# A decoder step on one Trainium2 core: the order of TensorE's work inside each attention step

## The chip, the cores and the metric

The program runs on one core of a Trainium2 chip. The metric is device time in microseconds (us), as the median of several executions. Three executions of the kernel before took 2781.90, 2783.97 and 2784.48 us, so the median is 2783.97 us.

TensorE appears as two rows in the profile: PE is the matrix product that streams through the array, PEld is the load of the stationary operand ahead of it. DVE is VectorE, ACT is ScalarE, POOL is GpSimd, SP issues transfers.

## The reference, cut to what matters

Two layers are computed for a prompt of 1024 tokens and for 8 short sample sequences of 8 tokens. The change touches only the attention of the second layer. In it, each of 16 heads of the prompt computes

```
s = q @ k.T * Dh**-0.5 - slope * distance        # causal, three dilation patterns
p = exp(s - max(s));  den = sum(p)
o = (p @ v) / den
```

and each sample sequence does the same for 8 new queries against a cache of 2048 keys and values, of which the kernel reads ten tiles of 128 positions each (`cache_k`, `cache_v`). The three patterns are folded into one additive bias (log of how often a key is counted), so one softmax per head is enough.

## The kernel before, in words

**Steps.** The 16 heads are taken as 8 pairs, and each pair's 1024 queries in 8 blocks of 128. That makes 64 prompt steps, numbered n = 0 to 63, with qb = n mod 8 the query block. Step n handles (qb + 1) * 128 key columns for both heads, so steps grow from qb = 0 to qb = 7. Two more steps (64, 65) finish the pipeline, and five steps (-5 to -1) run ahead of it. The first four of them are slipped between the matrix products of the q/k/v projection (line 483).

**The pipeline of the prompt.** In step n TensorE computes the scores of block n (`scores`, line 2419, 64 rows of the array for each head). VectorE adds the bias and takes the maximum (line 2679). ScalarE takes the exponential (`probs`, line 2585, once for each head, e = 0 and 1). In step n+1 TensorE turns the probabilities (transposes, line 2459, in units of up to four 128x128 blocks), and VectorE copies each turned unit out of PSUM (line 2638, `att_pt`). In step n+2 TensorE multiplies them with the values (`pv`, lines 2501 and 2505, the array split into two halves of 64 columns), ScalarE copies a row of reciprocal sums (line 2607), and VectorE writes the result (line 2710, `att_out`). `pv(n-2)`, called in step n, waits for two things of VectorE's step n-1: for the last turned unit of block n-2 (`t_out`), and for `att_out` of block n-3, which is the last instruction that VectorE has in step n-1 (`a_ox`).

**The samples.** One sample sequence is spread over eight steps, s = 0 to 7, and s = (qb + 5) mod 8 until the last pair, where s = 6 and 7 move to steps 58 and 60. Its key tiles are turned (line 2444) in two units each. `K_AT` says at which unit each s begins. ScalarE copies every unit out (line 2561, `smp_kt`, room for two tiles). A turned tile is multiplied with the queries (`tile_scores`, line 2472, the array split into four parts of 32 columns), at the places that `SCORED` names by (s, f). In s = 7 the ten value tiles are used (`sample_pv`, line 2526, also split in four), at the places of `WEIGHED`.

**Order.** Nothing is scheduled by a planner: every engine runs the list that is written out. A step has four phases, f = 1 to 4, and the units of a step (`turns`) are dealt out two to a phase. TensorE's list in a phase is: `scores` (f = 1 only), the phase's transposes, `pv` (f = 1 only), `tile_scores`, `sample_pv`.

**Banks.** A turned unit needs one PSUM bank, and the unit is not started before the copy of the unit that had the bank last. Two banks are always there. Two more are the second halves of the scores' banks: `rest` (line 2311) allows them in steps with qb under 4 in every phase, and in the others from phase 3, after VectorE has read the scores. The scores of the next step in turn wait for the copies out of those two banks before they write their second half.

**Memory.** Key and value tiles come by DMA into ten or twelve buffers. A buffer is loaded again when its key tile has been turned or its value tile has been used.

Of the kernel before, what the change touches and what calls it, by code (L numbers as in the profile page):

```python
# [25 lines left out]
QT = SEQ // P  # L26
# [106 lines left out]
def build(nc, a):  # L133
# [2114 lines left out]
    NSLOT = HP * QT  # L2248
# [10 lines left out]
    def sample_slot(n):  # L2259
        b, s = divmod(n + LEAD, 8)  # L2260
        if n >= min(LAST_S.values()) or b >= DB or slot_of(b, s) != n:
            b, s = DB - 1, next((s for s, x in LAST_S.items() if x == n), None)
        return (b, s) if s is not None else (None, None)

    K_AT = (0, 4, 8, 11, 14, 17, 20, 20, 20)
    SCORED = {(0, 2): (0,), (0, 3): (1,), (1, 2): (2,), (1, 3): (3,), (2, 2): (4,), (3, 1): (5,), (3, 3): (6,), (4, 2): (7,),
              (5, 1): (8,), (5, 3): (9,)}
    WEIGHED = {(7, 1): range(1, 5), (7, 2): range(5, 8), (7, 4): (8, 9, 10, 0)}

    def turns(n):  # L2270

# [18 lines left out]
    def by_act(unit):  # L2290

        return unit[0] not in ("p", "s") or unit[0] == "s" and unit[2] == 1

    def phase(n, f):

        nt = len(turns(n))
        return range(2 * f - 2, min(2 * f, nt) if f < 4 else nt)
# [10 lines left out]
    for n in SLOTS:  # L2308
        for f in range(1, 5):
            for i in phase(n, f):  # L2310
                rest = () if n < 0 else (2,) if n >= NSLOT else (2, 3) if n % QT < 4 or f >= 3 else ()
                x = min((0, 1) + rest, key=lambda b: last_use[b])
                last_use[x] = len(TB_)
                TC_.append(TB_.count(x) + 1)
                TB_.append(x)
# [85 lines left out]
    def att_pe(pe):  # L2401
# [129 lines left out]
        def step(n, f):  # L2531
            b, s = sample_slot(n)
            if 0 <= n < NSLOT and f == 1:
                scores(n)
            for i in phase(n, f):
                turn(n, i)
            if 2 <= n and f == 1:
                pv(n - 2)
            for t in SCORED.get((s, f), ()):
                tile_scores(b, t)  # L2540
            sample_pv(b, WEIGHED.get((s, f), ()))

        return step

# [35 lines left out]
    def s9_act(act):  # L2580
        def probs(n, e):
            W = (n % QT + 1) * P
            k = 2 * (n % 4) + e
            act.wait_ge(a_red, 2 * n + e + 1)
            act.activation(SX[n % 2][:, e, 0:W], SX[n % 2][:, e, 0:W], ACT.Exp, bias=NBM[:, k:k + 1], scale=-1.0,
                           accum_out=DEN[:, k:k + 1]).then_inc(a_p, 1)

        for n in SLOTS[N_RUN + LEAD:]:
            b, s = sample_slot(n)
            mine = [i for i, u in enumerate(turns(n)) if by_act(u)]  # L2590
            for i in mine[0:2]:
                take_act(act, n, i)
            if 0 <= n < NSLOT:
                probs(n, 0)
            for i in mine[2:3]:
                take_act(act, n, i)
            if 0 <= n < NSLOT:
                probs(n, 1)
            for i in mine[3:]:
                take_act(act, n, i)  # L2600
            if n == NSLOT + 1:
                act.wait_ge(a_red, 2 * NSLOT)
                for k in range(3):
                    out1_hi(act, k)
            if 2 <= n:
                act.wait_ge(a_o, n - 1)
                act.activation(RS[:, n % 2, :], PS[:, 6, P:2 * P], ACT.Copy).then_inc(a_rc, 1)
            if s == 5:
                act.wait_ge(b_mn, b + 1)
                act.activation(SS[:, :], SS[:, :], ACT.Exp, bias=NMN[:, 0:1], scale=-1.0,  # L2610
                               accum_out=DNS[:, 0:1]).then_inc(b_p, 1)
            if n == slot_of(DB - 1, 7) + 2:
                act.wait_ge(b_oc, DB)
                for e in range(2):
                    act.activation(ODUP[:, :, e, :], OALL[:, :].rearrange("p (b d) -> p b d", b=DB),
                                   ACT.Copy).then_inc(b_du, 1)
            if n == NSLOT - 5:
                split_hi(act, B_OUT1)

    def s9_dve(dve):  # L2620
# [28 lines left out]
        def piece(b, i):  # L2649
            c, w = (0, 2 * P) if i < 5 else (2 * P, DS)  # L2650
            k = 0 if i == 5 else i
            dve.wait_ge(b_sc, 5 * b + k + 1)
            dve.tensor_tensor_reduce(SS[:, i * 256:i * 256 + w], PS[:, 7, c:c + w], BSS[:, i * 256:i * 256 + w],
                                     -(DH ** -0.5), 3.0e38, ALU.add, ALU.min, NM6[:, i:i + 1]).then_inc(b_red, 1)
# [10 lines left out]
        for n in SLOTS:  # L2665
            b, s = sample_slot(n)
            units = turns(n)
# [19 lines left out]
            if n == slot_of(DB - 1, 7) + 1:  # L2687
                weigh(DB - 1)
            for f in range(1, 5):
                for i in range(2 * f - 2, min(2 * f, len(units)) if f < 4 else len(units)):  # L2690
                    if units[i][0] == "qk" or not by_act(units[i]):
                        take(n, i)
                for t in SCORED.get((s, f), ()):
                    if t % 2:
                        piece(b, t // 2)
                    if t == 1:
                        piece(b, 5)
            if s == 5:
                dve.wait_ge(b_red, 6 * b + 6)
                dve.tensor_reduce(NMN[:, :], NM6[:, :], AX.X, ALU.min).then_inc(b_mn, 1)  # L2700
# [285 lines left out]
```

## Time and profile before

| | us |
|---|---|
| median of three executions | 2783.97 |
| profiled execution, its own time | 2784.42 |
| span of the profile | 2782.6 |
| attention, first `scores` to the last product of `pv` | 1504.2 to 1929.1 |

The profiled execution took 1.8 us more than its span; it is 0.45 us above the median. The whole program keeps TensorE busy for 98% of the span. The attention is 425 us of it, of which the first pair of heads takes 55.6 us, the next six together 320.5 us, and the last pair with the two closing steps 48.8 us. Times in the trace are microseconds from the start of the span. An entry such as [0.17 <-issue] behind a row is idle time of that engine right before it, with what ended it; "issue" means that nothing the profile shows was waited for.

### The profile page before, as it was taken

The page shows a single profiled execution, that of the slowest core. Times are in us where ns is not written, and L with a number is a line of the kernel's source. Part 1 is how long each engine was busy: PE and PEld are TensorE (multiplying, and loading weights), DVE is VectorE, ACT ScalarE, POOL GpSimd, SP SyncE. Part 2 cuts the span into 40 slices and gives each one's busy share as a digit, 9 for nine tenths or more (in the row PEclk, how much of TensorE's full clock was granted, in tenths as well). Part 3 has the DMA queues.
Part 4 walks back from the last instruction along what each step waited for, and adds up shares of the span by engine and source line. Part 5 has one row for each costly group of instructions (what it writes and reads, how often), then busy time and mean ns, then how long its engine had stood idle before and what let it go on. Part 6 is the DMA issues. An engine that isn't in the chain of part 4 may idle for free.

```text
span 2782.6 us, 54662 instructions
## 1 busy us (share of the span) xinstructions
PE 2739.0 (98%) x23577; PEld 2618.6 (94%) x23577; DVE 1737.1 (62%) x2858; ACT 946.1 (34%) x1690; POOL 118.5 (4%) x220
## 2 busy tenths in 40 slices
PE   7999999999999999999999999999999999999998
PEld 7999999999999999999997777777999999999998
DVE  5754536877777776755512566556377767776676
ACT  5543513322222222422223555555232222222222
POOL 1010000000000000000011111110000000000000
PEclk9999999999999999999999999999999999999999
DMA  5120220111111111232356776873101111111112
GB/s 200 37 80 18 67 92 30 32 60 47 47 46 46 46 46 47 85 112 85 95 176 212 237 258 220 266 253 129 61 16 46 46 46 47 46 47 46 53 55 80
DMA packets 126381, 254.53 MB, mean 91 GB/s; under 512 B 7617, under 2 KB 88725, under 8 KB 125632
## 3 DMA queue, kind: packets, MB, share of 16 engines
q1 hardware_dynamic: 112944, 189.26, 21.0%
q0 software_dynamic: 11888, 57.25, 5.9%
q8 instruction: 189, 3.10, 0.5%
q10 hardware_dynamic: 1312, 4.52, 0.5%
q14 instruction: 48, 0.39, 0.0%
HBM read 222.98 MB, written 28.02 MB: 90 GB/s over the span
## 4 chain that ended last, share of the span: by engine, by line
PE 92%; DVE 4%; ACT 2%; DMA 1%; issue 1%; POOL 0%; ACTq 0%; POOLq 0%; DVEq 0%
PE psum L1574 30%; PE psum L1629 17%; PE psum L483 14%; PE psum L224 11%; PE psum L1549 3%; PE psum L2444 3%; PE psum L2501 2%; PE psum L2419 2%; PE psum L2459 2%; PE psum L2472 1%; PE psum L2526 1%; DMA x_natural<-in_x_prompt 1%; DMA cache_tile<-in_cache_k 1%; PE psum L592 1%; PE psum L2448 1%
## 5 line engine op out<-in xcount | busy, mean ns | idle before, releaser
L1810 DVE TENSOR_TENSOR x_res<-x_res,psum 128x544 f32<-128x544 f32 x352 | 250.5, 719 | 155.5 <-PE psum L1629 155.5
L483 PE MATMUL psum<-w_hi,h_hi 128*128 128x256 f32 (+1 forms) x1152 | 327.2, 284 | 1.0 <-ACT qkv_tok L2074 1.0
L483 PE MATMUL psum<-w_hi,h_lo 128*128 128x256 f32 (+1 forms) x1152 | 323.6, 281 | 0.0
L483 PE MATMUL psum<-w_lo,h_hi 128*128 128x256 f32 (+1 forms) x1152 | 323.0, 280 | 0.0
L1629 PE MATMUL psum<-ffn_hi,ffn_unit_hi 128*128 128x272 f32 x1408 | 292.6, 289 | 1.8 <-DVE x_res L1810 1.5
L1629 PE MATMUL psum<-ffn_lo,ffn_unit_hi 128*128 128x272 f32 x1408 | 291.5, 288 | 0.0
L1629 PE MATMUL psum<-ffn_hi,ffn_unit_lo 128*128 128x272 f32 x1408 | 290.7, 288 | 0.0
L1574 PE MATMUL psum<-h_hi,ffn_unit_lo 128*128 128x272 f32 x1280 | 265.2, 288 | 0.0
L1574 PE MATMUL psum<-h_lo,ffn_unit_hi 128*128 128x272 f32 x1280 | 264.8, 288 | 0.0
L1574 PE MATMUL psum<-h_hi,ffn_unit_hi 128*128 128x272 f32 x1280 | 264.5, 288 | 0.0
L1629 PEld LDWEIGHTS psum<-ffn_hi,ffn_unit_hi 128*128 128x128 f32 x1408 | 220.7, 188 | 3.2 <-DVE x_res L1810 3.2
L1629 PEld LDWEIGHTS psum<-ffn_lo,ffn_unit_hi 128*128 128x128 f32 x1408 | 220.8, 188 | 0.0
L1629 PEld LDWEIGHTS psum<-ffn_hi,ffn_unit_lo 128*128 128x128 f32 x1408 | 220.7, 188 | 0.0
L483 PEld LDWEIGHTS psum<-w_hi,h_hi 128*128 128x128 f32 (+1 forms) x1152 | 215.1, 187 | 4.6 <-issue 2.2
L483 PEld LDWEIGHTS psum<-w_lo,h_hi 128*128 128x128 f32 (+1 forms) x1152 | 215.2, 187 | 0.0
L483 PEld LDWEIGHTS psum<-w_hi,h_lo 128*128 128x128 f32 (+1 forms) x1152 | 215.0, 187 | 0.0
L1574 PEld LDWEIGHTS psum<-h_hi,ffn_unit_hi 128*128 128x128 f32 x1280 | 201.0, 188 | 0.0
L1574 PEld LDWEIGHTS psum<-h_hi,ffn_unit_lo 128*128 128x128 f32 x1280 | 200.7, 188 | 0.0
L1574 PEld LDWEIGHTS psum<-h_lo,ffn_unit_hi 128*128 128x128 f32 x1280 | 200.6, 189 | 0.0
L1574 PE MATMUL psum<-ffn_t_hi,ffn_unit_lo 128*128 128x272 f32 x960 | 198.6, 288 | 0.0
L1574 PE MATMUL psum<-ffn_t_hi,ffn_unit_hi 128*128 128x272 f32 x960 | 198.6, 288 | 0.0
L1574 PE MATMUL psum<-ffn_t_lo,ffn_unit_hi 128*128 128x272 f32 x960 | 198.5, 288 | 0.0
(385 smaller groups left out, 5307.1 us busy)
## 6 DMA issues: line engine op xcount, KB each, us to landing
cache_tile<-in_cache_k SPq DMA_DIRECT2D x64, 512.0 KB, 8.5
cache_tile<-in_cache_v SPq DMA_DIRECT2D x64, 512.0 KB, 11.9
w_raw<-in_w_ffn_gate SPq DMA_DIRECT2D x22, 1024.0 KB, 5.1
w_raw<-in_w_ffn_up SPq DMA_DIRECT2D x22, 1024.0 KB, 5.1
w_raw<-in_w_ffn_down SPq DMA_DIRECT2D x22, 1024.0 KB, 4.9
w_raw<-in_w_in_att SPq DMA_DIRECT2D x12, 1024.0 KB, 7.1
w_raw<-in_w_in_rec SPq DMA_DIRECT2D x10, 1024.0 KB, 5.0
park_x<-x_res POOLq DMA_DIRECT2D x2, 4368.0 KB, 13.3
```

The source lines that it names most:

```text
L224: mm = pe.matmul(PS[:, bank + c, 0:n], st[slot][:, wc:wc + P], mv[:, k, c * CW:c * CW + n], start=(i < NCH), stop=(i >= 3 * NCH * nk - NCH))
L483: mm = pe.matmul(PS[0:n, bank, 0:BW], st[:, k, w:w + n], mv[slot][:, k * BW:(k + 1) * BW], start=(k == 0 and x == 0) if used is None else ...
L592: pe.matmul(PS[:, bank, 0:n], wt[:, j, :], XC[j % 2][:, c * CW:c * CW + n], start=True, stop=True).then_inc(g_in, 1)
L1549: mm = pe.matmul(PS[:, 2 * s + c, 0:CC], st[slot][:, k * BW + f * P:k * BW + (f + 1) * P], mv[:, k, t * TH + c * CC:t * TH + (c + 1) * CC] ...
L1574: mm = pe.matmul(PS[:, 2 * s + c, 0:CC], st[i % NU][:, k * P:(k + 1) * P], mv[:, k0 + k, t * TH + c * CC:t * TH + (c + 1) * CC], start=(fr ...
L1629: mm = pe.matmul(PS[:, 2 * s + c, 0:CC], st[(w0 + m // 2) % NU][:, x:x + P], mv[:, f, t * TH + c * CC:t * TH + (c + 1) * CC], start=(n < 2 ...
L1810: dve.tensor_tensor(x, x, pset(dset(g, i)), ALU.add).then_inc(s_res, 1)
L2419: mm = pe.matmul(PS[:, 2 * e + c // 512, 0:min(512, W - c)], q[p % 2][e * DH:(e + 1) * DH, qb * P:(qb + 1) * P], k[p % 2][e * DH:(e + 1) * ...
L2444: mm = pe.transpose(to[:, h * P:(h + 1) * P], TILE[BUF[j]][:, hp * P:(hp + 1) * P], ident[:, :])
L2448: mm = pe.transpose(to[:, t * P:(t + 1) * P], (QN, KN)[c // 2][:, 4 * (c % 2) + t, :], ident[:, :])
L2459: mm = pe.transpose(to[:, (k - c) * P:(k - c + 1) * P], SX[x % 2][:, e, y * P:(y + 1) * P], ident[:, :])
L2501: pe.matmul(PS[e * DH:(e + 1) * DH, 6, 0:P], VN[p % 2][:, x, e * DH:(e + 1) * DH], PT[:, m % 2, e * (qb + 1) + x, :], start=(x == 0), stop ...
```

## The change

In every phase TensorE now does the column-split products first (`pv`, `tile_scores`, `sample_pv`) and the transposes last. Every tile is scored in phase 1 of the step after the one that turned it, two tiles at a time. All the key units are turned in s = 0 to 4, four a step. Value tiles are used in two groups instead of three. The two further banks are allowed from phase 2. ScalarE takes the exponential of head 0 before its first two copies (it was after them), and VectorE does the maxima of the sample scores before its copies of turned units.

```diff
-    K_AT = (0, 4, 8, 11, 14, 17, 20, 20, 20)
-    SCORED = {(0, 2): (0,), (0, 3): (1,), (1, 2): (2,), (1, 3): (3,), (2, 2): (4,), (3, 1): (5,), (3, 3): (6,), (4, 2): (7,),
-              (5, 1): (8,), (5, 3): (9,)}
-    WEIGHED = {(7, 1): range(1, 5), (7, 2): range(5, 8), (7, 4): (8, 9, 10, 0)}
+    K_AT = (0, 4, 8, 12, 16, 20, 20, 20, 20)
+    SCORED = {(1, 1): (0, 1), (2, 1): (2, 3), (3, 1): (4, 5), (4, 1): (6, 7), (5, 1): (8, 9)}
+    WEIGHED = {(7, 1): range(1, 6), (7, 3): (6, 7, 8, 9, 10, 0)}
...
-                rest = () if n < 0 else (2,) if n >= NSLOT else (2, 3) if n % QT < 4 or f >= 3 else ()
+                rest = () if n < 0 else (2,) if n >= NSLOT else (2, 3) if n % QT < 4 or f >= 2 else ()
...
                 scores(n)
-            for i in phase(n, f):
-                turn(n, i)
             if 2 <= n and f == 1:
                 pv(n - 2)
             for t in SCORED.get((s, f), ()):
                 tile_scores(b, t)
             sample_pv(b, WEIGHED.get((s, f), ()))
+            for i in phase(n, f):
+                turn(n, i)
...
+            if 0 <= n < NSLOT:
+                probs(n, 0)
             for i in mine[0:2]:
                 take_act(act, n, i)
             if 0 <= n < NSLOT:
-                probs(n, 0)
-            for i in mine[2:3]:
-                take_act(act, n, i)
-            if 0 <= n < NSLOT:
                 probs(n, 1)
-            for i in mine[3:]:
+            for i in mine[2:]:
                 take_act(act, n, i)
...
-                for i in range(2 * f - 2, min(2 * f, len(units)) if f < 4 else len(units)):
-                    if units[i][0] == "qk" or not by_act(units[i]):
-                        take(n, i)
                 for t in SCORED.get((s, f), ()):
                     if t % 2:
                         piece(b, t // 2)
                     if t == 1:
                         piece(b, 5)
+                for i in range(2 * f - 2, min(2 * f, len(units)) if f < 4 else len(units)):
+                    if units[i][0] == "qk" or not by_act(units[i]):
+                        take(n, i)
```

TensorE, kernel before, step 15 (qb = 7) behind its scores, and the scores of step 16. `cache_tile` rows are key tiles being turned, `att_scores` rows are probabilities being turned, `att_pt` and `att_diag` are `pv`, `smp_kt` is `tile_scores`:

```order
L2444 MATMUL psum<-ident,cache_tile_191 128x128 x8
L2501 MATMUL psum<-att_pt,att_v_218 64x128 x12
L2505 MATMUL psum<-att_diag,ones 64x128 x2
L2444 MATMUL psum<-ident,cache_tile_182 128x128 x4
L2459 MATMUL psum<-ident,att_scores_207 128x128 x4
L2472 MATMUL psum<-smp_kt,smp_q_blocks 32x128 x8
L2459 MATMUL psum<-ident,att_scores_207 128x128 x10
L2419 MATMUL psum<-att_k_hi_203,att_q_hi_199 128x128 x2
L2419 MATMUL psum<-att_k_lo_205,att_q_hi_199 128x128 x2
L2419 MATMUL psum<-att_k_hi_203,att_q_lo_201 128x128 x2
```

TensorE, changed kernel, the same step, then the scores and the `pv` of step 16 (line numbers are one lower):

```order
L2500 MATMUL psum<-att_pt,att_v_218 64x128 x12
L2504 MATMUL psum<-att_diag,ones 64x128 x2
L2471 MATMUL psum<-smp_kt,smp_q_blocks 32x128 x16
L2443 MATMUL psum<-ident,cache_tile_191 128x128 x8
L2443 MATMUL psum<-ident,cache_tile_183 128x128 x8
L2458 MATMUL psum<-ident,att_scores_207 128x128 x14
L2418 MATMUL psum<-att_k_hi_203,att_q_hi_199 128x128 x2
L2418 MATMUL psum<-att_k_lo_205,att_q_hi_199 128x128 x2
L2418 MATMUL psum<-att_k_hi_203,att_q_lo_201 128x128 x2
L2500 MATMUL psum<-att_pt,att_v_218 64x128 x14
L2504 MATMUL psum<-att_diag,ones 64x128 x2
```

The eight transposes that stood between `scores` and `pv` are gone from there, the two kinds of transposes are one row of 30, and one more key unit and one more tile product are in the step.

ScalarE, kernel before, step 15: copies of turned key units (`smp_kt`), the exponentials of both heads, and the row of reciprocal sums:

```order
L2561 ACTIVATE smp_kt<-psum 128x512 x2
L2585 ACTIVATE att_scores_208,att_den<-att_scores_208,att_max 128x1024
L2561 ACTIVATE smp_kt<-psum 128x512
L2585 ACTIVATE att_scores_208,att_den<-att_scores_208,att_max 128x1024
L2607 ACTIVATE att_rden_rows<-psum 128x128
```

ScalarE, changed kernel, the same step:

```order
L2584 ACTIVATE att_scores_208,att_den<-att_scores_208,att_max 128x1024
L2560 ACTIVATE smp_kt<-psum 128x512 x2
L2584 ACTIVATE att_scores_208,att_den<-att_scores_208,att_max 128x1024
L2560 ACTIVATE smp_kt<-psum 128x512 x2
L2604 ACTIVATE att_rden_rows<-psum 128x128
```

The first exponential now stands ahead of all copies; the second still stands between the copies of the second and the third key unit, and one copy has been added behind it.

## Rows read from the trace of the kernel before

**Rows 1.** The page: busy us of the engines, share of the span, instructions.

```profile
PE 2739.0 (98%) x23577; PEld 2618.6 (94%) x23577; DVE 1737.1 (62%) x2858; ACT 946.1 (34%) x1690; POOL 118.5 (4%) x220
```

**Rows 2.** Stretches of attention: length, busy times, granted clock, DMA share, GB/s.

```profile
1504.20:1559.80 55.60, 50.50 (x613) 37.98 (x609) 28.60 (x83) 29.95 (x67) 10.02 (x19) 0.94 0.93 302
1559.80:1880.30 320.50, 318.36 (x4149) 245.56 (x4148) 192.85 (x547) 171.37 (x402) 53.58 (x100) 1.00 0.73 245
1880.30:1929.10 48.80, 45.05 (x557) 35.02 (x556) 36.01 (x90) 25.47 (x57) 6.05 (x10) 1.00 0.46 158
```

**Rows 3.** Waits in the attention, 1504 to 1929: us in total, times, longest.

```profile
PEld psum L2444 <- issue: 17.6, 64, 2.9
...
PEld psum L2501 <- issue: 11.0, 62, 0.6
...
PEld psum L2472 <- ACT smp_kt L2561: 5.6, 16, 1.8
```

**Rows 4.** Timeline of PEld, one step with qb = 7: start, length, operation, count.

```profile
1711.73 0.19 PEld L2419 LDWEIGHTS psum<-att_k_hi,att_q_hi 64*128 64x128 f32 x2 [0.20 <-issue]
...
1713.32 0.86 PEld L2444 LDWEIGHTS psum<-ident,cache_tile 128*128 128x128 f32 x8 [0.36 <-issue]
1714.34 1.29 PEld L2501 LDWEIGHTS psum<-att_pt,att_v 128*64 128x64 f32 x24 [0.17 <-issue]
...
1717.04 0.38 PEld L2472 LDWEIGHTS psum<-smp_kt,smp_q_blocks 128*32 128x32 f32 x16 [0.17 <-issue]
1717.62 1.07 PEld L2459 LDWEIGHTS psum<-ident,att_scores 128*128 128x128 f32 x10 [0.20 <-issue]
1718.86 0.19 PEld L2419 LDWEIGHTS psum<-att_k_hi,att_q_hi 64*128 64x128 f32 x2 [0.17 <-issue]
...
1719.34 0.86 PEld L2444 LDWEIGHTS psum<-ident,cache_tile 128*128 128x128 f32 x8
```

**Rows 5.** Timeline of ACT in the same step.

```profile
1714.01 1.09 ACT L2561 ACTIVATE smp_kt<-psum 128x512 f32<-128x512 f32 x2 [2.27 <-PE psum L2444]
1714.99 1.15 ACT L2585 ACTIVATE att_scores<-att_scores,att_max 128x1024 f32<-128x1024 f32 x1
...
1717.21 1.14 ACT L2585 ACTIVATE att_scores<-att_scores,att_max 128x1024 f32<-128x1024 f32 x1
...
1718.34 0.26 ACT L2607 ACTIVATE att_rden_rows<-psum 128x128 f32<-128x128 f32 x1
```

**Rows 6.** Timeline of DVE at the end of the same step.

```profile
1718.31 1.62 DVE L2638 COPY att_pt<-psum 128x512 f32<-128x512 f32 x3
1719.85 0.28 DVE L2710 TENSOR_TENSOR att_out<-psum,att_rden_rows 128x128 f32<-128x128 f32 x1
```

**Rows 7.** Groups on ACT, 1504 to 1929: exponentials of two widths.

```profile
L2585 ACT ACTIVATE att_scores<-att_scores,att_max 128x1024 f32<-128x1024 f32 x16 | 18.3, 1145 | 0.0
...
L2585 ACT ACTIVATE att_scores<-att_scores,att_max 128x768 f32<-128x768 f32 x16 | 14.9, 931 | 6.3 <-DVE att_max L2679 6.3
```

**Rows 8.** Timeline of DVE, end of step 56 and start of step 57.

```profile
1885.39 1.89 DVE L2638 COPY att_pt<-psum 128x512 f32<-128x512 f32 x3 [3.34 <-PE psum L2459]
...
1888.20 0.28 DVE L2710 TENSOR_TENSOR att_out<-psum,att_rden_rows 128x128 f32<-128x128 f32 x1
```

**Rows 9.** Timeline of PEld, end of step 56 and start of step 57.

```profile
1884.64 1.34 PEld L2459 LDWEIGHTS psum<-ident,att_scores 128*128 128x128 f32 x12
...
1887.31 0.19 PEld L2419 LDWEIGHTS psum<-att_k_hi,att_q_hi 64*128 64x128 f32 x2 [0.17 <-issue]
...
1887.86 0.20 PEld L2459 LDWEIGHTS psum<-ident,att_scores 128*128 128x128 f32 x2
1888.60 0.99 PEld L2501 LDWEIGHTS psum<-att_pt,att_v 128*64 128x64 f32 x18 [0.54 <-DVE att_pt L2638]
```

**Rows 10.** Timeline of PEld, steps 2 and 3.

```profile
1517.02 0.20 PEld L2505 LDWEIGHTS psum<-att_diag,ones 128*64 128x64 f32 x4 [0.77 <-POOL att_diag L2765]
...
1526.54 0.50 PEld L2444 LDWEIGHTS psum<-ident,cache_tile 128*128 128x128 f32 x3 [2.88 <-issue]
```

## The prediction

> **What bounds the kernel now.** The page comes first: TensorE is busy for 98% of the span, the others for 62% or less [rows 1], so time moves only where TensorE's own list gets shorter or where it waits. The second view cuts the attention into stretches. The six middle pairs of heads take 320.5 us with TensorE busy for 318.4 and the granted clock at 1.00; VectorE works 60% and ScalarE 53% of it [rows 2]. The third view is the waits: there is hardly one on another engine. What idles is the weight load with the releaser "issue", 11.0 us in 62 places before `pv` alone [rows 3]. The timeline of one step shows where: between two transposes of a row there is no gap, but wherever the array's split changes (64-row scores, full transposes, 64-column `pv`, 32-column tile products) there is one of 0.17 to 0.20 us [rows 4]. So the attention is bound by TensorE's instructions plus the changes of split, and the change is about the latter. The Trainium skill says in "TensorEngine Tiling (Array Packing)", Key Properties, that changing the tiling mode, not just the tile, drains TensorE; the trace agrees with its 0.17 us.
>
> **What it saves.** I counted the changes of split in both orders of TensorE, from the first score product to the last product of `pv`: 374 before, 243 after, about 49 and 31 per pair. By their kinds (0.17 where a transpose or `pv` ends, 0.20 where a tile product or the scores end, [rows 4]) the 131 that go are worth 23.3 us. In the steps ahead of step 0 seven more go, 1.3 us. Sum -24.6. The step from scores to `pv` is new in 62 places. The trace has only the step from scores to transposes, whose load idles 0.36 us at the widest block, most of that behind the product that is still streaming [rows 4]. I price it like the one it replaces; at no cost the sum would be 12 lower, at twice 0.20 it would be 12 higher.
>
> A tile product now comes a step after its transposes, so it no longer waits for ScalarE's copy: 5.6 us in 16 waits, of which 16 x 0.17 is drain that stays counted above, -2.9 [rows 3], and I estimate -1.4 for the like in the lead steps. The number of products, transposes, copies and exponentials is unchanged, and so are the bytes moved.
>
> **What it adds: waits.** The handovers first. A transpose takes 0.107 us (8 in 1.02 less the 0.17 of drain), a unit of four 0.43 [rows 4]. Its copy starts 0.69 us after the unit does, on ScalarE (1713.32 to 1714.01) as on VectorE (1717.62 to 1718.31). ScalarE copies a unit every 0.49 and the last is done after 0.60; its exponential with its reading takes 1.13 for 1024 columns [rows 5] and 0.11 less for every 128 fewer [rows 7]. VectorE copies one every 0.60, half a unit in 0.34, and `att_out` takes 0.28 [rows 6, 8]. From the end of `att_out` to the waiting `pv` it is 0.12 [rows 8, 9].
>
> *Seventh unit.* With four banks the seventh transposed unit needs the bank of the third key unit. Take 0 as the start of the first key unit. ScalarE copies two, from 0.69 to 1.67, then runs its second exponential to 2.80, and only then copies the third, done at 3.40. TensorE, with no other work between, is there at 6 x 0.43 = 2.58: 0.82 us of wait at qb = 7, 0.71 at qb = 6, 0.60 at qb = 5. The eighth unit (qb = 7) waits for the fourth copy, 3.89, another 0.06. Before, a tile product and the pair of transposes ahead of `pv` lay between and there was no such wait.
>
> *pv at qb = 0.* The eighth unit (two blocks) ends at 4.10, the drain 0.17 and the narrow scores 0.48 [rows 4] bring TensorE to `pv` at 4.75. VectorE copies the seventh from 4.09 and the eighth from 4.69, and `att_out` ends at 5.31, with 0.12 of handover: 0.68 of wait. Before, eight transposes (1.02 us) stood ahead of `pv` and covered it. Queued behind the waiting `pv` is all the rest of the step.
>
> *pv at qb = 1.* In the step before, all four units are probabilities and all go to VectorE. From their start it needs 0.69 + 4 x 0.60 + 0.06 for the least of the sample scores + 0.28 + 0.12 = 3.55. TensorE needs 16 x 0.107 + 0.17 + 0.55 (the scores of 256 columns, [rows 9]) = 2.43: 1.12 of wait. Step 57 of the kernel before shows this very wait: it has no key units ahead of `pv`, only two transposes, and `pv` stood 0.54 us for VectorE [rows 9].
>
> *The rest, by the same working.* At qb = 1 the two query units hold their banks until ScalarE and then VectorE have read them, 0.59; `pv` at qb = 2 then waits 0.75 for VectorE's long list of that step; at qb = 4 the second half of the scores and `pv` wait 0.32 together, at qb = 5 0.05. Per pair: 0.82 + 0.06 + 0.71 + 0.60 + 0.68 + 1.12 + 0.59 + 0.75 + 0.32 + 0.05 = 5.7 us, against about 18 x 0.175 = 3.1 us that the same pair saves in drains. Six full pairs give 34.2, the first pair from its step 4 on 2.6, the last in its first two steps 1.8: +38.6. In the closing steps, without key units, waits like these are there already (3.75 of the 48.8 us are not busy, [rows 2]); I leave them even.
>
> **Start and transfers.** In step 2 `pv` waits for POOL [rows 10], whose list is held by the last stores of the projection. That moment doesn't move, so what TensorE saves between the projection and it is lost, and slightly more work stands behind it: +3. The next wait, 2.88 us at step 3 [rows 10], is for the first key tile of the second sample. Its buffer is freed by the first value tile, and now about 1.6 us more work lies between the two: -2. The same spacing, 7.8 us in place of 6.2, holds for every later sample, so SP's loads, with the DMA engines 73% busy [rows 2], are not later than now.
>
> **Sum.** -24.6 - 4.3 - 2 + 38.6 + 3 = +10.7 on the profiled execution's own 2784.42, so 2795, 11 above the median of 2783.97. VectorE then works no more than before and still has slack on average; what costs is the order.
>
> **Rivals.**
> *Drains only.* If copies and waits stay hidden, the kernel gains 24.6 + 4.3 + 2 less 3 and comes to 2757. The drains [rows 4] and the 98% [rows 1] speak for it. Against it stands step 57 [rows 9], and the handovers above are read from rows and leave the copies no room. The Trainium skill ("TensorEngine Tiling (Array Packing)") stands on both sides: its rule on mode switches makes every removed switch a gain and would lead here, while its section PSUM Bottleneck says that tiling speeds up TensorE but not the emptying of PSUM. Chance 0.10; together with halfway cases in which under 60% of the waits appear (38.6 x 0.6 = 23.2, so 2780 or less: under 2778.4), faster has 0.16.
> *A draw.* With 60 to 85% of the waits (a copy that starts earlier than the step I read, or waits that overlap: one wait moves VectorE's start of the next step and softens the next) the sum is -5 to +5: 2779 to 2789. Chance 0.19.
> *The clock falls.* In the first stretch, with its long waits, the granted clock is 0.94 against 1.00 later [rows 2]. If the new idle time, 5.7 us of waits in 55, did the same everywhere, 6% of the 320 us would add 19: 2814. Against it: the last stretch has 3.75 us not busy in 48.8 and its clock is 1.00. Chance 0.04.
> *The new split costs double.* Scores to `pv` at 0.40 in place of 0.20: 2807. Nothing in the rows says so; 0.06.
> The forecast case itself (2789 to 2802) has 0.55.
>
> **How the numbers follow.** A measurement of this kernel tells about 0.2%, 5.6 us, from no change. Faster by more than that takes the first rival with its halfway cases, 0.16; within it the draw, 0.19; slower the forecast and the last two, 0.65. The range of 8 in 10 runs from 2777 to 2807: it leaves out most of the faster cases and the clock. The likeliest case's own range is 2789 to 2802.
>
> **What would show it.** In the changed profile: weight loads of `pv` with a releaser on VectorE (`att_out` or `att_pt`), worst at qb = 1 with about 1.1 us, then qb = 2 and 0; probability transposes at qb = 5 to 7 that wait for ScalarE's `smp_kt` by 0.6 to 0.8; "issue" gaps fewer by a third; no wait of tile products; six middle pairs of 56 us each instead of 53.4; the granted clock 1.00 in them. Middle pairs under 53 us would refute the handovers; pairs at 50 would mean the drains are all there is.

## The result and the profile after

The changed kernel takes 2806.48 us (median of 6 runs, 2802.86 to 2807.82), the kernel before 2784.52 (6 runs beside it, 2781.90 to 2787.15). The ratio is 1.0077 with a 95% interval of 1.0068 to 1.0087: 22 us slower. The forecast was 2795.0 in a range of 2777 to 2807, so direction and cause were foreseen, and the loss was put at half its size.

The profiled execution took 2806.05 us, its span 2804.2. The page answers to [rows 1]: the share of TensorE fell from 98% to 97%, with the same number of instructions.

```profile
PE 2730.4 (97%) x23577; PEld 2621.8 (93%) x23577; DVE 1739.2 (62%) x2858; ACT 947.4 (34%) x1690; POOL 118.8 (4%) x220
```

The stretches of the changed kernel, with the columns of [rows 2]: the first pair of heads, the six middle pairs, the fourth pair alone, and the last pair with the closing steps. They are cut at the first score product of a step.

```profile
1502.12:1557.15 55.03, 47.93 (x608) 37.55 (x607) 28.65 (x82) 30.19 (x68) 9.24 (x17) 0.97 0.92 298
1557.15:1899.53 342.38, 312.94 (x4148) 248.14 (x4148) 194.61 (x547) 171.88 (x402) 53.73 (x100) 1.00 0.68 228
1672.42:1728.55 56.13, 51.90 (x692) 41.27 (x691) 32.45 (x92) 28.62 (x67) 9.24 (x17) 1.00 0.70 235
1899.53:1949.91 50.38, 43.70 (x545) 33.74 (x544) 36.04 (x89) 24.25 (x54) 6.07 (x10) 1.00 0.44 153
```

The fourth pair of the kernel before:

```profile
1665.86:1718.86 53.00, 52.94 (x692) 40.92 (x692) 32.14 (x92) 28.56 (x67) 9.22 (x17) 1.00 0.74 250
```

The whole loss lies in the middle pairs: 342.4 against 320.5 us, +21.9, where TensorE has 29 us without a product in place of 2. I call the fourth pair regular, because nothing but the written order delays it: 56.13 against 53.00, +3.1. Six times that is 18.8. The other 3.1 are stops that come only in some pairs (below), net of those that the kernel before had. The granted clock is 1.00 in all middle pairs, as before.

The waits in the attention, as in [rows 3] (total us, times, longest):

```profile
PEld psum L2500 <- DVE att_pt L2635: 25.4, 26, 1.8
...
PEld psum L2458 <- issue: 18.7, 35, 0.9
...
PEld psum L2500 <- issue: 9.0, 26, 1.3
PEld psum L2443 <- issue: 8.0, 29, 2.1
```

Key transposes had 17.6 us of gaps in 64 places [rows 3] and now have 8.0 in 29: most of that is drains that went. New at this size is the first row, `pv` waiting for VectorE. In the kernel before it is 2.3 us in three places, all in the last pair and the closing steps:

```profile
PEld psum L2501 <- DVE att_pt L2638: 2.3, 3, 1.4
```

The wait of tile products for ScalarE, 5.6 us [rows 3], has no row any more. Over all lines the "issue" gaps went from 326 to 245, but their sum from 71.7 to 75.4 us, since some of them are waits for a bank and not drains.

Which waits these are shows in the weight loads of TensorE in the fourth pair. First the steps with qb = 7 and 0, to be held against [rows 4]:

```profile
1719.80 0.19 PEld L2418 LDWEIGHTS psum<-att_k_hi,att_q_hi 64*128 64x128 f32 x2 [0.17 <-issue]
...
1720.65 0.19 PEld L2418 LDWEIGHTS psum<-att_k_hi,att_q_hi 64*128 64x128 f32 x2 [0.33 <-DVE att_pt L2635]
...
1721.54 1.29 PEld L2500 LDWEIGHTS psum<-att_pt,att_v 128*64 128x64 f32 x24 [0.36 <-issue]
...
1724.23 1.73 PEld L2443 LDWEIGHTS psum<-ident,cache_tile 128*128 128x128 f32 x16 [0.20 <-issue]
1725.93 0.90 PEld L2458 LDWEIGHTS psum<-ident,att_scores 128*128 128x128 f32 x8
1727.70 0.69 PEld L2458 LDWEIGHTS psum<-ident,att_scores 128*128 128x128 f32 x6 [0.86 <-issue]
1728.55 0.19 PEld L2418 LDWEIGHTS psum<-att_k_hi,att_q_hi 64*128 64x128 f32 x2 [0.17 <-issue]
...
1729.73 0.34 PEld L2500 LDWEIGHTS psum<-att_pt,att_v 128*64 128x64 f32 x6 [0.77 <-DVE att_pt L2635]
```

Six units of transposes run without a gap, then the seventh stands for 0.86 us, and in the next step `pv` stands for 0.77. The new step from scores to `pv` idles 0.36, exactly what scores to transposes idled [rows 4]. ScalarE in the same step, against [rows 5]:

```profile
1722.92 1.15 ACT L2584 ACTIVATE att_scores<-att_scores,att_max 128x1024 f32<-128x1024 f32 x1 [3.13 <-DVE att_max L2676]
...
1724.93 1.09 ACT L2560 ACTIVATE smp_kt<-psum 128x512 f32<-128x512 f32 x2 [0.76 <-PE psum L2443]
1725.90 1.15 ACT L2584 ACTIVATE att_scores<-att_scores,att_max 128x1024 f32<-128x1024 f32 x1
...
1727.03 1.08 ACT L2560 ACTIVATE smp_kt<-psum 128x512 f32<-128x512 f32 x2
```

The third key unit is copied from 1727.03 on, behind the second exponential, and the seventh transposed unit begins at 1727.70, 3.47 us after the first; the working gave 3.40. Then `pv` at qb = 1 and 2 of the same pair, the two worst places:

```profile
1680.09 1.76 PEld L2500 LDWEIGHTS psum<-att_pt,att_v 128*64 128x64 f32 x32 [1.25 <-DVE att_pt L2635]
...
1686.67 0.23 PEld L2500 LDWEIGHTS psum<-att_pt,att_v 128*64 128x64 f32 x4 [0.92 <-DVE att_pt L2635]
```

What was not foreseen shows in step 13. TensorE is in the second half of its scores, between products that wait for nothing:

```profile
1590.24 0.19 PEld L2418 LDWEIGHTS psum<-att_k_hi,att_q_hi 64*128 64x128 f32 x2 [0.32 <-ACT smp_kt L2560]
1592.75 0.19 PEld L2418 LDWEIGHTS psum<-att_k_lo,att_q_hi 64*128 64x128 f32 x2 [2.32 <-issue]
```

Packets of the queues between 1586 and 1592 us (packets, MB, share of the 16 DMA engines):

```profile
q1 hardware_dynamic: 482, 1.43, 100.9%
q8 instruction: 1, 0.02, 1.4%
```

The DMA engines are full with cache tiles, and one packet of the instruction queue lies among them. It starts at 1590.0 and takes 1.4 us: it is under way when the stop begins (1590.4) and over 1.3 us before TensorE goes on. At step 37 TensorE stops for 1.28 us between its scores and `pv`, the DMA engines are full there too (103.2% for q1 between 1755 and 1762), and TensorE goes on 1.7 us after the end of such a packet. That alone proves little: the six middle pairs have 34 such packets, one in about 10 us, and 17 of them lie among full DMA engines, but only these two stand beside a stop of over a microsecond. One that starts at 1707.1, in the regular fourth pair, stops nothing. The kernel before has 34 too, 16 of them among full DMA engines, and no stop of that length. Step 3 is another matter: its 2.08 us are a wait for a key tile, for the product's row there names the DMA transfer of `cache_tile` as its releaser.

The Trainium skill ("Runtime: NRT & Kernel Launch", the note on `TENSOR_LOAD` in The ~15µs preamble/postamble breakdown) says that instructions are fetched on their own, without an instruction for it. The trace agrees in that only the packet shows.

### The profile page after: what moved, and what is told of

Same layout as the page of the kernel before. It is cut to its first block, busy times and chain, and to the rows that moved or that the text cites. A ratio compares the mean times of both kernels' runs of the same rounds, so it can differ in the third digit from the quotient of the medians.

```text
span 2804.2 us, 54662 instructions
## 1 busy us (share of the span) xinstructions
PE 2730.4 (97%) x23577; PEld 2621.8 (93%) x23577; DVE 1739.2 (62%) x2858; ACT 947.4 (34%) x1690; POOL 118.8 (4%) x220
## 4 chain that ended last, share of the span: by engine, by line
PE 89%; DVE 5%; DMA 2%; ACT 2%; issue 1%; POOL 0%; ACTq 0%; SPq 0%; DVEq 0%; POOLq 0%
PE psum L1574 29%; PE psum L1629 17%; PE psum L483 14%; PE psum L224 11%; PE psum L1549 3%; PE psum L2443 3%; PE psum L2500 2%; PE psum L2418 2%; PE psum L2458 2%; PE psum L2471 1%; DVE att_pt L2635 1%; PE psum L2525 1%; DMA cache_tile<-in_cache_k 1%; DMA x_natural<-in_x_prompt 1%; PE psum L592 1%
```

## The experiments

"Pair" is the fourth pair of heads, regular in every kernel here; "six pairs" are the middle ones. Both are read from one profiled run each. The ratios are to runs of the kernel before that were taken beside each kernel; their medians lie between 2783.03 and 2784.52 us.

| kernel | median us (range) | ratio to before, 95% | pair | six pairs |
|---|---|---|---|---|
| before | 2784.52 | | 53.00 | 320.5 |
| changed | 2806.48 | 1.0068 to 1.0087 | 56.13 | 342.4 |
| e1 exponentials first | 2794.18 (2792.8 to 2795.7) | 1.0023 to 1.0048 | 55.16 | 334.1 |
| e2 tile products ahead | 2797.07 (2794.9 to 2800.1) | 1.0033 to 1.0058 | 55.22 | 336.0 |
| e3 two units ahead | 2779.49 (2775.9 to 2782.4) | 0.9972 to 0.9990 | 52.60 | 321.0 |
| e4 changed, quarter of cache | 2798.51 (2798.1 to 2798.7) | 1.0035 to 1.0066 | 56.12 | 337.3 |
| e5 before, ScalarE as changed | 2795.04 (2794.0 to 2800.2) | 1.0031 to 1.0056 | 54.82 | 329.9 |
| e6 e1 and e2 | 2786.59 (2785.1 to 2790.0) | 1.0003 to 1.0021 | 54.08 | 326.3 |
| e7 e3, other banks | 2784.00 (2779.0 to 2785.5) | 0.9990 to 1.0007 | 53.53 | 322.9 |
| e8 before, quarter of cache | 2779.42 (2777.8 to 2783.4) | 0.9975 to 0.9993 | 53.00 | 318.2 |
| e9 changed, ScalarE as before | 2829.33 (2826.7 to 2830.9) | 1.0151 to 1.0179 | 58.83 | 359.0 |
| e10 e3, quarter of cache | 2775.16 (2770.9 to 2776.3) | 0.9954 to 0.9979 | 52.60 | 316.0 |

**e1: both exponentials ahead of all copies.**

```diff
                 probs(n, 0)
-            for i in mine[0:2]:
-                take_act(act, n, i)
-            if 0 <= n < NSLOT:
                 probs(n, 1)
-            for i in mine[2:]:
+            for i in mine:
                 take_act(act, n, i)
```

> The changed kernel with one thing altered: ScalarE takes both exponentials of a step ahead of all its copies. Theory of the handovers: the seventh transposed unit no longer waits for the third key unit's copy, so the gaps of 0.65, 0.75 and 0.86 us at qb = 5, 6 and 7 go, while the waits of the value products at qb = 0, 1 and 2 (0.7, 1.1 and 0.7 us) stay. That is 2.26 us a pair, 7 pairs, 16 us: 2806.5 becomes about 2790 (2786 to 2795). Rival, that the lost time is in transfers and late instructions or in a costlier change of split: no change, 2803 to 2810.

It came to 2794.18, 12.3 less than the changed kernel and inside the first theory's bounds. The weight loads at the end of qb = 7 and at qb = 0:

```profile
1719.70 1.59 PEld L2458 LDWEIGHTS psum<-ident,att_scores 128*128 128x128 f32 x14
1721.46 0.18 PEld L2418 LDWEIGHTS psum<-att_k_hi,att_q_hi 64*128 64x128 f32 x2 [0.17 <-issue]
...
1722.98 0.13 PEld L2500 LDWEIGHTS psum<-att_pt,att_v 128*64 128x64 f32 x1 [1.11 <-DVE att_pt L2632]
```

The 14 probability transposes run through, so the gap of 0.86 was the wait for ScalarE's third copy. But `pv` at qb = 0 now stands 1.11 in place of 0.77: TensorE is there sooner and VectorE isn't. The second half of the scores stands longer as well, 0.66 at qb = 6 (nothing before) and 0.64 at qb = 7 (0.33 before). A pair gains 0.97 where the three gaps held 2.26. So the mechanism is shown, but that the time fell inside the bounds is in part luck: the theory had seven pairs gain 16 us, six gain 5.8 by their regular part, and the rest of the 12.3 is fewer stops and time gained outside the middle pairs.

**e2: tile products ahead of `pv`, the 243 changes of split kept.**

```diff
-            if 2 <= n and f == 1:
-                pv(n - 2)
             for t in SCORED.get((s, f), ()):
                 tile_scores(b, t)
+            if 2 <= n and f == 1:
+                pv(n - 2)
```

> The changed kernel with one thing altered: in phase 1 the two tile products stand ahead of the value products, not behind. The number of changes of split stays 243. Theory of the handovers: the 1.0 us of tile products covers VectorE's tail at qb = 0, 4, 5 and 7, where the value products waited 0.69, 0.37, 0.16 and 0.15 us; at qb = 1 and 2, which have no tile product, the waits of 1.1 and 0.7 us stay. 1.37 us a pair, 7 pairs: 2806.5 becomes about 2797 (2794 to 2801). Rival, that the step from scores to value products is itself the costly new split (62 places, now 27): 35 places fewer at 0.2 us more each would give 7 us beyond that, below 2792. Rival of transfers: 2803 to 2810.

2797.07, as the first theory had it; the pair gains 0.91 of the 1.37 that it was to gain, and the rest comes from outside the regular steps. At qb = 0 the tile products cover VectorE's copies, at qb = 1 no tile product is there and the wait is unchanged:

```profile
1670.40 0.81 PEld L2471 LDWEIGHTS psum<-smp_kt,smp_q_blocks 128*32 128x32 f32 x32
1671.41 1.51 PEld L2500 LDWEIGHTS psum<-att_pt,att_v 128*64 128x64 f32 x28 [0.20 <-issue]
...
1676.87 0.23 PEld L2500 LDWEIGHTS psum<-att_pt,att_v 128*64 128x64 f32 x4 [1.25 <-DVE att_pt L2635]
```

**e3: two transposed units ahead of `pv` again.** TensorE does scores, tile products, two units, `pv`, the other units; ScalarE two copies, both exponentials, the rest. I counted 301 changes of split.

```diff
-            if 2 <= n and f == 1:
-                pv(n - 2)
             for t in SCORED.get((s, f), ()):
                 tile_scores(b, t)
+            if f == 1:
+                for i in phase(n, f):
+                    turn(n, i)
+            if 2 <= n and f == 1:
+                pv(n - 2)
             sample_pv(b, WEIGHED.get((s, f), ()))
-            for i in phase(n, f):
-                turn(n, i)
+            if f > 1:
+                for i in phase(n, f):
+                    turn(n, i)
```

> The changed kernel's tables, but the first two transposed units of a step stand ahead of the value products again, behind the tile products, and ScalarE copies two units, takes both exponentials and copies the rest. Changes of split: 301, against 374 before and 243 in the changed kernel. Theory of the handovers: nearly all waits are covered and 73 changes of split are saved against the kernel before: 2784.5 less 73 x 0.175 = 13 less about 3 for the removed waits of tile products, plus up to 5 for late transfers: 2771 (2766 to 2779), faster than both. Rival, that a change of split costs less than it looks because the weight load only idles where the product streams on: 2781 to 2788. Rival of transfers: above 2785.

2779.49, faster than both kernels (by 0.1 to 0.28% against before), though 8 us above the value expected and just outside its bounds. With 58 more changes of split it is 27 us faster than the changed kernel. The step with qb = 7:

```profile
1708.52 0.19 PEld L2418 LDWEIGHTS psum<-att_k_hi,att_q_hi 64*128 64x128 f32 x2 [0.50 <-DVE att_pt L2638]
...
1710.42 0.86 PEld L2443 LDWEIGHTS psum<-ident,cache_tile 128*128 128x128 f32 x8 [0.20 <-issue]
1711.44 1.29 PEld L2500 LDWEIGHTS psum<-att_pt,att_v 128*64 128x64 f32 x24 [0.17 <-issue]
...
1713.12 0.86 PEld L2443 LDWEIGHTS psum<-ident,cache_tile 128*128 128x128 f32 x8 [0.17 <-issue]
1713.94 0.90 PEld L2458 LDWEIGHTS psum<-ident,att_scores 128*128 128x128 f32 x8
1715.01 0.69 PEld L2458 LDWEIGHTS psum<-ident,att_scores 128*128 128x128 f32 x6 [0.16 <-issue]
```

`pv` waits for no more than a drain, and the seventh unit, where no split changes, for 0.16. What is left is the second half of the scores, which waits 0.50 for the copies out of its bank, and the like at qb = 4 and 6.

**e4: the changed kernel with less cache traffic.** From the second sample on, 256 of the 1024 columns of each cache tile are loaded; the outputs of those samples are not the reference's.

```diff
-                sp.dma_start(TILE[BUF[j]][:, :], src[name][:, b, t, :])...
+                q = D if b < 1 or BUF[j] >= 10 else 256
+                sp.dma_start(TILE[BUF[j]][:, 0:q], src[name][:, b, t, 0:q])...
```

> The changed kernel, but for the second sample onward only a quarter of each cache tile's columns is loaded (256 of 1024), so the outputs of those samples are not the reference's. Everything else is as in the changed kernel. Theory of the handovers: only the irregular gaps go that the regular step lengths don't explain, 5.6 us at steps 13, 21, 37, 45 and 51 and up to 3.9 us at step 3: 2797 (2795 to 2802), and the regular waits at qb = 5 to 2 stay as they are. Rival, that the transfers are what makes the changed kernel slower: below 2790.

2798.51, 8.0 less than the changed kernel, and the runs lie within 0.6 us in place of 5. Its fourth pair takes what it took with all the traffic; its six pairs are 5.1 shorter:

```profile
1555.64:1892.89 337.25, 311.80 (x4147) 247.98 (x4146) 194.75 (x547) 171.79 (x402) 53.74 (x100) 1.00 0.31 95
1668.09:1724.21 56.12, 51.90 (x692) 41.27 (x691) 32.45 (x92) 28.63 (x67) 9.24 (x17) 1.00 0.32 96
```

So the stops inside TensorE's rows come with the traffic, and the regular waits don't. How traffic stops TensorE is not shown by this.

**e5: the kernel before with ScalarE's new order alone.**

```diff
-            for i in mine[0:2]:
-                take_act(act, n, i)
             if 0 <= n < NSLOT:
                 probs(n, 0)
-            for i in mine[2:3]:
+            for i in mine[0:2]:
                 take_act(act, n, i)
             if 0 <= n < NSLOT:
                 probs(n, 1)
-            for i in mine[3:]:
+            for i in mine[2:]:
```

> The kernel before with one part of the change alone: ScalarE takes the exponential of head 0 ahead of its first two copies of turned key units, and the second ahead of the third copy. TensorE and VectorE keep their old order. Theory: the copies then come up to 1.13 us later, and in the old order a tile product follows its copies within the same step (16 such waits, 5.6 us in all, are there already), so in the steps with s = 0, 1, 2 and 4 about 1 us of new wait each, some 3 us a pair: 2800 us (2790 to 2810). This part of the change was then only possible together with tile products a step later. Rival: ScalarE is busy for a third of the time only and its order doesn't matter by itself: 2783 to 2786.

2795.04: slower by 11.1, inside the first theory's bounds, though a pair loses 1.8 and not 3. It isn't the tile products alone. The key units of phase 2 wait for their bank too, as in this step with qb = 7:

```profile
1724.53 0.25 PEld L2505 LDWEIGHTS psum<-att_diag,ones 128*64 128x64 f32 x4
1725.40 0.42 PEld L2444 LDWEIGHTS psum<-ident,cache_tile 128*128 128x128 f32 x4 [0.62 <-ACT smp_kt L2561]
```

**e6: e1 and e2 together.**

> The changed kernel with both earlier edits: both exponentials ahead of all of ScalarE's copies (alone it took the time to 2794.18), and the tile products ahead of pv (alone 2797.07). The changes of split stay at 243. Theory: the first edit's gain was partly handed on to pv at qb = 0, which waited 1.11 us for VectorE's copies; with two tile products standing ahead of that pv the wait is covered, so the two gains add or do better: 2783 us (2780 to 2787), and a regular pair of about 54.2 us in place of 56.1. Rival: the waits are all one chain and the second edit only moves what the first has left: 2790 to 2794.

2786.59. The gains alone were 12.3 and 9.4, together 19.9 of 21.7: they add, nearly. The two sit at different places, and the handed-on wait of e1 at qb = 0 is covered:

```profile
1665.39 0.81 PEld L2471 LDWEIGHTS psum<-smp_kt,smp_q_blocks 128*32 128x32 f32 x32
1666.42 1.54 PEld L2500 LDWEIGHTS psum<-att_pt,att_v 128*64 128x64 f32 x28 [0.22 <-issue]
```

So of the 22 us, 20 go by order alone, with all 131 removed changes of split still removed. But what is left is no better than the kernel before: the saved drains still pay for waits, mainly at qb = 1 and 2.

**e7: e3, with the last two units of a step kept out of the scores' banks (qb = 3 to 6).**

```diff
+                late = i >= len(turns(n)) - 2 and 3 <= n % QT < 7
-                rest = ... (2, 3) if n % QT < 4 or f >= 2 else ()
+                rest = ... (2, 3) if not late and (n % QT < 4 or f >= 2) else ()
```

> The kernel with two turned units ahead of pv (2779.49 us), and one edit on banks: in the steps with qb = 3 to 6 the last two turned units may not take the second halves of the scores' banks, so that the scores of the next step find these banks read. That version still waited 0.44 us at qb = 4, 0.51 at qb = 6 and 0.50 at qb = 7 in the second half of the scores. Theory: these 1.45 us a pair go, 9.4 us in 6.5 pairs, and about a third comes back as waits of the last units for the two banks that are left: 2773 us (2769 to 2777). Rival: all comes back, since VectorE's copies are what is late and not the choice of the bank: 2778 to 2781.

2784.00: both theories missed. Not only all came back, but 4.5 us more. The scores no longer wait; the last unit does, here at qb = 3:

```profile
1688.74 0.20 PEld L2459 LDWEIGHTS psum<-ident,att_scores 128*128 128x128 f32 x2 [1.08 <-ACT smp_kt L2565]
```

That is 1.08 for 0.44 saved at the next step, and 0.58 and 0.59 at qb = 5 and 6 for 0.50 each. A bank withheld moves the wait from a place where TensorE comes late to one where it comes early.

**e8: the kernel before with a quarter of the cache** (the edit of e4; the outputs of the samples from the second on are not the reference's).

> The kernel before with a quarter of each cache tile loaded (256 of 1024 columns) from the second sample on; what is computed from the rest of those tiles is not the reference's. Twin of the same edit on the changed kernel, which took it from 2806.5 to 2798.5 us. Theory: TensorE's stops inside a row of its own instructions come from the DMA engines being full, in both kernels; before has 2.5 us of them in the middle pairs and 2.9 us at step 3, so 2779 us (2777 to 2781), and the changed kernel is 19.5 us slower than this twin: the part of the change's cost that has nothing to do with transfers. Rival: the old order suffers nothing from them and stays at 2783 to 2785, so that the whole 8 us that the changed kernel gained by less traffic were the change's doing.

2779.42, 4.6 less than before, as the theory said. Its six pairs:

```profile
1556.27:1874.50 318.23, 317.57 (x4147) 245.44 (x4146) 192.87 (x547) 171.38 (x402) 53.60 (x100) 1.00 0.34 101
```

e4 is 19.1 us above this twin. So about 19 of the change's 22 us have nothing to do with the traffic that was taken away. The other 3 would be traffic that costs the new order 8.0 where it cost the old one 4.6. That rest is barely clear of the noise: the interval of the 22 us alone is 19 to 24.

**e9: the changed kernel with ScalarE's old order** (the lines of e5 the other way round).

> The changed kernel with ScalarE's order as before: two copies of turned key units, exponential of head 0, a third copy, exponential of head 1, the rest. TensorE and VectorE stay as changed. Theory: in the changed order all transposes stand in a row, so what counts is when the copies are done; the old order does the third copy behind one exponential as well, but the fourth behind two, 1.1 us later, and only the eighth unit (qb = 7) needs it: about 1 us a pair more, and the second exponential isn't earlier either. 2812 us (2808 to 2818). Rival: the old order has its first copies 1.1 us sooner, which takes away the wait at the third and fourth unit, and nothing waits for the rest: 2798 to 2804; then the new order on ScalarE was itself a part of the loss.

2829.33, far above the 2812 expected and on the other side of the rival. The step with qb = 7:

```profile
1735.66 0.42 PEld L2458 LDWEIGHTS psum<-ident,att_scores 128*128 128x128 f32 x4 [0.86 <-issue]
1737.27 0.20 PEld L2458 LDWEIGHTS psum<-ident,att_scores 128*128 128x128 f32 x2 [1.20 <-issue]
```

The eighth unit waits 1.20, as expected. The miss is a wait for the same fourth copy that I had left out: its bank is one of the scores' too, and at qb = 5 the second half of the scores stands for it.

```profile
1713.01 0.19 PEld L2418 LDWEIGHTS psum<-att_k_hi,att_q_hi 64*128 64x128 f32 x2 [1.12 <-ACT smp_kt L2560]
```

A pair is 2.7 longer. ScalarE's new order costs 11 in the old order of TensorE (e5) and saves 23 in the new one.

**e10: e3 with a quarter of the cache** (again not the reference's outputs of those samples).

> The kernel with two turned units ahead of pv (2779.49 us), with a quarter of each cache tile loaded (256 of 1024 columns) from the second sample on; what is computed from the rest is not the reference's. Theory: its trace shows 2.0 and 2.2 us of TensorE stopping inside its own rows in steps 13 and 37, 1.0 at step 51 and 4.4 in steps 2 and 3; without the traffic these 9.6 us shrink to some 1.5: 2771.5 us (2769 to 2774), 8 less than the twin of the kernel before (2779.42). Rival: less traffic is worth the 4.6 us that it was worth to the kernel before: 2774.5 to 2777.

2775.16, 4.3 less than e3: the rival was right. The first theory took the stops of one profile for the kernel's mean. The six pairs fell by 5.0, but the attention began 2.3 later, at 1502.76 in place of 1500.43. Why it began later is open. So about 4 of the 8 us by which e3 missed its 2771 are traffic. For the other 4 the waits at the second half of the scores (1.45 us gross in a pair) stand in the trace, and they are more than enough.

The exchange of `att_out` between VectorE and `pv` through one bank was not taken away by itself: a second copy of it would have had to share a bank with what is being read, and that version wasn't run. Nor were three smaller parts of the change run alone: the two further banks from phase 2, VectorE's maxima ahead of its copies, and the new places of the units and value tiles.

## Why the prediction was right, and where not

**The drains (-24.6).** Right. The fourth pair has 18 fewer changes of split. Outside the idle entries of the weight loads it takes 43.2 us in both kernels; the idle entries come to 9.8 us before and 12.9 after. The waits after, gross, are 0.77, 1.25, 0.34, 0.34, 0.92, 0.44, 0.32, 0.65, 0.75, 0.86 and 0.33, together 6.97, of which 0.25 stands there in any case (`pv` behind the scores of qb = 2). The kernel before had waits in this pair too, 0.13 at a tile product and 0.44 at the second half of the scores of qb = 6:

```profile
1705.47 0.19 PEld L2419 LDWEIGHTS psum<-att_k_hi,att_q_hi 64*128 64x128 f32 x2 [0.44 <-DVE att_pt L2638]
```

That leaves 9.2 us of other gaps before and 6.2 after: 3.0 over 18 changes, 0.17 each, where 0.17 to 0.20 was read from [rows 4].

**The tile products' waits (-4.3).** Right, no row is left. In the steps ahead of the attention 2.6 us of such waits went, in four places, where 1.4 was estimated.

**The added waits (+38.6).** The mechanisms were right, place by place; us in a pair:

| place | forecast | measured gap |
|---|---|---|
| seventh and eighth unit, qb = 7 | 0.82 + 0.06 | 0.86 |
| seventh unit, qb = 6 and 5 | 0.71, 0.60 | 0.75, 0.65 |
| `pv`, qb = 0 and 1 | 0.68, 1.12 | 0.77, 1.25 |
| query units' banks, qb = 1 | 0.59 | 0.34 + 0.34 |
| `pv`, qb = 2 | 0.75 | 0.92 |
| second half of scores, qb = 4, 5, 7 | 0.32, 0.05, none | 0.44, 0.32, 0.33 |

The gap of `pv` at qb = 2 holds 0.25 that stands there in any case. The term that was sized too small is the last line: the second half of the scores waits for a bank at qb = 5 and 7 as well, so that these places came to at least 0.7 us a pair more than forecast. Against that, the wait of 0.44 at qb = 6, which the kernel before had and the working left out, is gone. With all places together a pair lost 3.1 us where 2.6 was forecast: 0.5 a pair, 3 us in six. e3 and e9 show the wait of the scores again, and there it decided.

**"SP's loads ... are not later than now."** From this the sum put traffic at nothing, and that is the step that failed as far as is known. I looked only at loads that a product waits for. Against regular pairs, the middle pairs held about 2.5 us of stops before and 5.6 after, in one profiled run each (+3.1). e4 with e8 gives 2.9 to 3.4 us between the medians, depending on which median of the kernel before is taken. Both point the same way, but the second is barely clear of the noise, and whether loads are in fact later was not looked at.

**Step 3 (-2) and the start.** The DMA wait of step 3 [rows 10] was to shrink by 2 and went from 2.88 to 2.08 us, with more spread over the step, so that steps 2 and 3 lose about as much beyond their regular length as before. Outside the middle pairs the forecast had about -4, and the spans show -0.3: attention starts 2.1 earlier, the first pair gains 0.5, the last loses 1.6, and 0.8 is lost behind it. About 2 of these 4 are the -2 of step 3; the rest I haven't traced.

Together: 3 for the waits in the regular pairs, 3 for the stops, 4 outside give, roughly, the 11 us between +10.7 and the +21.6 of the spans. The result lies only half a microsecond inside the upper end of the range, 2807, and none of these three was among the reasons for that end. So the direction and most of the mechanism were foreseen, and that the range held is in part luck.

**The rivals.** *Drains only* fell at [rows 9], as argued: the waits came in full. The rule of the Trainium skill ("TensorEngine Tiling (Array Packing)", Key Properties) that changing the tiling mode drains TensorE stands: the trace agrees with 0.17 us each. The section PSUM Bottleneck of that page of the Trainium skill says that the copies out of PSUM may become the bottleneck once TensorE is faster. That tells this kernel's story better, and the trace agrees with 25.4 us of `pv` waiting for copies. *The clock falls*: 1.00 in the middle pairs. *The new split costs double* named 2807, the right time for a wrong reason: scores to `pv` idles 0.36 at the widest block, not more than scores to transposes [rows 4]. Without the traces it would pass for confirmed. e2 speaks against it too: with tile products behind the scores in 35 of the 62 places, the time stayed above the 2792 that this rival needed.

## What to carry to other kernels

Before instructions of one kind are grouped, write down what each of them was covering: a transpose between scores and `pv` looks like two changes of split, 0.35 us, and hid up to 1.25 us of another engine's copies (the gap of `pv` at qb = 1). Group only as far as the consumer's handover stays covered; e3 kept half of the regrouping (301 of 374 to 243 changes) and was the only one of the full-traffic versions faster than before. An order on one engine has no price of its own: ScalarE's new one cost 11 us with one order of TensorE and saved 23 with the other.

## What the hardware showed

- TensorE stopped 1.3 to 2.3 us between its own products, waiting for no semaphore, while the DMA engines were full (100.9% for q1) and a packet of the instruction queue had come 1.3 to 1.7 us before it went on (steps 13 and 37 here and in e3). With a quarter of the cache traffic all such stops of the middle pairs went, and the runs' spread shrank from 5 us to 0.6 (e4). That the packet is the cause is a guess: 15 others came among full DMA engines without such a stop. Why the new order seems to pay 8.0 us for the traffic and the old one 4.6 stays open.
- What a change of the array's split leaves idle goes by what stood before it: 0.17 us behind full transposes and `pv`, 0.20 behind tile products. Behind the scores it is no gap at all at qb = 0, 0.25 at qb = 2 and 6 and 0.36 at qb = 3 and 7, whether transposes, tile products or `pv` follow. Behind `sample_pv` it is 0.41, as in the fourth pair of the changed kernel:

```profile
1689.58 0.86 PEld L2447 LDWEIGHTS psum<-ident,att_k 128*128 128x128 f32 x8 [0.41 <-issue]
```

- The number of changes alone predicts nothing: 243, 301 and 374 changes took 2806.48, 2779.49 and 2784.52 us.
